# Two-layer decoder trunk: from a two-tile, two-layer order to a layer-by-layer order over nine tiles, with background weight conversion

## What is computed

```
for l in range(2):
    x = x + 0.5 * swiglu(rms_norm(x), ffn1)             # F1: 1024 -> 2816 -> 1024
    h = rms_norm(x); q, k, v, u = h @ w_in[l]           # M: 1280 columns
    x = x + cat(norm(window_attn(q, k, v)), norm(pool(u))) @ w_out[l]
    x = x + cross_attention(rms_norm(x), rms_norm(mem)) # 4 heads, 256 memory rows
    x = x + 0.5 * swiglu(rms_norm(x), ffn2)             # F2
return rms_norm(x)
```

## Time and profile before

| | |
|---|---|
| median of 6 runs | 6290.85 us |
| the profiled execution, its own time | 6285.33 us |
| span of its slowest core (core 5) | 6283.7 us (cores 6255.7 to 6283.7) |
| mean granted TensorE clock, all cores | 0.930 to 0.933 |
| TensorE busy | 5334.3 us, 85% of the span, 28528 matmuls |
| VectorE, ScalarE, GpSimd busy | 38%, 27%, 16% |
| DMA queue of SP, share of 16 engines | 40.9% |
| DMA queue of GpSimd, share of 16 engines | 11.5% |
| matmul waits for FFN slots that are cast at first use | 425.1 us |
| HBM read, written | 1005 MB, 104 MB |

### The profile page before, as it was taken

The page is one execution under the profiler, slowest core; times in us unless marked ns, Lnnn a source line. Parts: engine busy times, 40 slices in busy tenths (PEclk is TensorE's granted clock), DMA queues, the critical chain, the costliest instruction groups (busy, mean ns, idle before and its releaser), DMA issues.

```text
span 6283.7 us, 87478 instructions; the slowest of 8 cores (6255.7 to 6283.7 us)
## 1 busy us (share of the span) xinstructions
PE 5334.3 (85%) x28528; PEld 2782.1 (44%) x28528; DVE 2379.3 (38%) x4167; ACT 1690.3 (27%) x3070; POOL 978.5 (16%) x1154
## 2 busy tenths in 40 slices
PE   5555756696765999999999999999999999999988
PEld 2222322243322444445455555555555555555545
DVE  1231222141122354434445444344444354453452
ACT  1132111122212232223233233233332332332342
POOL 1111111111101112111122111111211111110111
PEclk9777878898877999999999999999999999999999
DMA  8534457545364445444455655555555555555554
GB/s 194 133 85 114 117 123 159 132 138 151 101 150 101 173 141 189 138 162 156 162 196 168 210 180 188 170 196 179 199 176 187 180 187 197 187 171 190 178 164 163
DMA packets 280504, 1019.35 MB, mean 162 GB/s; under 512 B 32336, under 2 KB 32704, under 8 KB 279808
## 3 DMA queue, kind: packets, MB, share of 16 engines
q1 hardware_dynamic: 239472, 870.52, 40.9%
q0 software_dynamic: 39440, 141.12, 11.5%
q10 hardware_dynamic: 1152, 2.10, 0.1%
HBM read 1005.22 MB, written 104.33 MB: 177 GB/s over the span
## 4 chain that ended last, share of the span: by engine, by line
PE 68%; DMA 12%; DVE 8%; issue 5%; ACT 5%; POOL 1%; DVEq 0%; ACTq 0%; POOLq 0%; SPq 0%
PE ps L328 68%; DMA sb_fr<-wf 7%; DVE sb_hM L421 2%; DVE sb_hF L421 2%; DMA sb_mr<-wx 2%; DMA sb_mr<-wm 1%; ACT sb_rst L148 1%; DMA wfb<-sb_fr 1%; ACT sb_sqf L148 1%; ACT sb_tmp L148 1%; DVE sb_x L501 1%; POOL sb_ach L393 1%; ACT sb_pT L148 1%; POOL sb_acc L393 0%; ACT L145 0%
## 5 line engine op out<-in xcount | busy, mean ns | idle before, releaser
L328 PE MATMUL ps<-sb_hF,sb_fr 128*128 128x384 bf16 (+1 forms) x14080 | 2718.0, 350 | 248.4 <-DMA sb_fr<-wf 197.5
L328 PEld LDWEIGHTS ps<-sb_hF,sb_fr 128*128 128x128 bf16 x14080 | 1394.9, 100 | 1476.3 <-issue 437.5
L328 PE MATMUL ps<-sb_act,sb_fr 128*128 128x384 bf16 (+1 forms) x7040 | 1421.9, 356 | 234.6 <-DMA sb_fr<-wf 227.6
L466 DVE TENSOR_TENSOR sb_act<-ps,sb_sg 128x384 bf16<-128x384 f32 (+1 forms) x880 | 524.0, 596 | 1917.0 <-PE ps L328 1425.9
L393 POOL TENSOR_TENSOR sb_acc<-sb_acc,sb_sqf 128x384 f32<-128x384 f32 (+2 forms) x592 | 644.3, 1091 | 3386.9 <-ACT sb_sqf L148 3378.7
L328 PEld LDWEIGHTS ps<-sb_act,sb_fr 128*128 128x128 bf16 x7040 | 700.8, 101 | 883.1 <-issue 368.7
L328 PE MATMUL ps<-sb_hM,sb_mr 128*128 128x384 bf16 (+1 forms) x4000 | 862.4, 355 | 165.2 <-DMA sb_mr<-wm 99.0
L148 ACT ACTIVATE sb_sg<-ps 128x384 f32<-128x384 f32 (+1 forms) x880 | 454.0, 519 | 1310.3 <-PE ps L328 1157.2
L328 PEld LDWEIGHTS ps<-sb_hM,sb_mr 128*128 128x128 bf16 x4000 | 398.0, 100 | 569.8 <-issue 295.5
L148 ACT ACTIVATE sb_sqf<-sb_x 128x384 f32<-128x384 f32 (+1 forms) x630 | 345.0, 553 | 1124.3 <-DVE sb_x L501 360.8
L148 ACT ACTIVATE sb_pT<-ps 128x512 bf16<-128x512 f32 (+2 forms) x452 | 234.1, 553 | 522.9 <-PE ps L328 520.8
(11 more groups left out here) (86 smaller groups left out, 2326.8 us busy)
## 6 DMA issues: line engine op xcount, KB each, us to landing
sb_fr<-wfb SPq DMA_DIRECT2D x1188, 512.0 KB, 4.1
sb_mr<-wmb SPq DMA_DIRECT2D x162, 512.0 KB, 5.2
sb_mr<-wab SPq DMA_DIRECT2D x160, 512.0 KB, 4.4
sb_fr<-wf POOLq DMA_DIRECT2D x132, 512.0 KB, 8.6
wfb<-sb_fr SPq DMA_DIRECT2D x132, 512.0 KB, 5.3
sb_mr<-wx POOLq DMA_DIRECT2D x32, 512.0 KB, 9.7
sb_x<-xT POOLq DMA_DIRECT2D x7, 1536.0 KB, 11.6
yT<-sb_x POOLq DMA_DIRECT2D x56, 192.0 KB, 6.5
```

What stands on the lines that cost most here:

```text
L328: P.op("pe", lambda h: h.matmul(out_ap, lt, rh, start=st, stop=sp_, skip_group_check=True), reads=list(rb), writes=(ob_,), signal=(i == n ...
L466: P.op("dve", lambda h: h.tensor_tensor(out=actF[:, hc, :T], in0=d[1][0][:, :T], in1=sg[si][:, :T], op=ALU.mult), (d[1][1], sgb[si]), (act ...
```

## The change

Tiles are now nine (six of 512 positions, three of 384), and the order is by layer: the 18 (layer, tile) units v = 0 to 17 run in one pipeline, whose stage v has F2 of unit v-1, M of unit v and F1 of unit v+1. Stage -1 is F1 of unit 0, stage 18 is F2 of unit 17. After layer 0 x goes to DRAM (`store_x`) and is loaded again for layer 1; the rope tables go the same way. F1 of every unit takes its norm statistics from x in `xs` (`prenorm_steps`), spread over the F2 down projection and the attention.

Only `wf[0]` (33 slots, F1 of layer 0) is still cast into the ring at first use. All other weights are cast DRAM to DRAM by `convert`, several slots per DMA on the POOL queue, and every load of them is a bf16 load on SP. `conv_first` (25 slots: wm 0 to 4, wx 0 to 15, wm 5 to 8 of layer 0) is issued at the end of stage -1, `conv_second` (33 slots, F2 of layer 0) spread over stage 0, and the 91 slots of layer 1 spread over stages 1 to 7. The DMAs that write `wab` get a semaphore for each ring slot.

```diff
-    n += n % 2
...
+    wxb_d = nc.dram_tensor("wxb", [L, 16, 128, SLOT], BF16, kind="Internal").ap()
+    x1_d = nc.dram_tensor("x1", [128, NCH, NT], F32, kind="Internal").ap()
+    tab_d = nc.dram_tensor("tab", [ntl, 2, 128, TT], F32, kind="Internal").ap()
...
-            if (a, s) not in fresh[kind]:
-                fresh[kind].add((a, s))
+            src, dst, buf = BANKS[kind]
+            if kind == "wf" and a == 0 and s not in fresh:
+                fresh.add(s)
                 P.dma("pool", slot[:, :], src[a, s], writes=(sb_,), box=swbox[rk][i])
...
+        def convert(kind, a, s0, s1):
+            src, dst, buf = BANKS[kind]
+            P.dma("pool", dst[a, s0:s1].rearrange("s p e -> (s p) e"), src[a, s0:s1].rearrange("s p e -> (s p) e"),
+                  writes=tuple(buf[a][s0:s1]), box=P.new_box(f"cv_{kind}{a}_{s0}"))
...
-            P.dma("pool", xs[s][:, :, :T], xT_d[:, :, c0:c0 + T], writes=tuple(xbs[s]), box=xbox[s])
+            s = v % NXS
+            src, rd = (xT_d, ()) if l == 0 else (x1_d, (x1buf[ti],))
+            P.dma("pool", xs[s][:, :, :T], src[:, :, c0:c0 + T], reads=rd, writes=tuple(xbs[s]), box=xbox[s])
+
+        def store_x(ti, l):
+            c0, T = tiles[ti]
+            s = (l * ntl + ti) % NXS
+            P.dma("pool", x1_d[:, :, c0:c0 + T], xs[s][:, :, :T], reads=tuple(xbs[s]), writes=(x1buf[ti],), box=xsbox[s])
...
+            if l < L - 1:
+                return [(lambda: store_x(ti, l), 0.1)]
...
+        conv_first = conv_list("wm", 0, 0, 5, 3) + conv_list("wx", 0, 0, 16, 4) + conv_list("wm", 0, 5, 9, 4)
+        conv_second = conv_list("wf", 1, 0, 33, 3)
+        conv_later = []
+        for l in range(1, L):
+            conv_later += conv_list("wf", 2 * l, 0, 33, 3) + conv_list("wm", l, 0, 9, 3) + conv_list("wx", l, 0, 16, 4) + conv_list("wf", 2 * l + 1, 0, 33, 3)
...
+        for v in range(-1, NV_T + 1):
+            M = tl(v) if 0 <= v < NV_T else None
+            F2 = tl(v - 1) if v - 1 >= 0 else None
+            F1 = tl(v + 1) if v + 1 < NV_T else None
...
+                fs += raw(gu2[:2]) + early
+                fs += merge(gu2[2:], seg1)
+                ps_, ph_ = prenorm_steps(*F1)
+                fs += sprinkle(merge(dn2, seg2), raw(ps_ + ph_))
+                fs += raw(gu1[:2])
...
+                fs += merge(gu1[2:], final_steps(*F2) + [(lambda v=v: load_x(v + 2), 0.1)] + segw + seg3)
+                d1, d2 = split_frac(dn1, 0.72)
+                fs += merge(d1, seg4)
+                fs += merge(d2, tail)
+                run(sprinkle(fs, bg))
```

More of the change, by code:

```diff
@@ L368, in load, with conv_list @@
                 flush_wb(rk, 0)
-                P.dma("sp", slot[:, :], dst[a, s], reads=(buf[a][s],), writes=(sb_,))
+                rd = tuple(buf[a][4:]) if kind == "wab" and s >= 4 else (buf[a][s],)
+                P.dma("sp", slot[:, :], dst[a, s], reads=rd, writes=(sb_,))
             return slot, sb_
+        def convert(kind, a, s0, s1):
+            src, dst, buf = BANKS[kind]
+            P.dma("pool", dst[a, s0:s1].rearrange("s p e -> (s p) e"), src[a, s0:s1].rearrange("s p e -> (s p) e"),
+                  writes=tuple(buf[a][s0:s1]), box=P.new_box(f"cv_{kind}{a}_{s0}"))
+        def conv_list(kind, a, s0, s1, step):
+            return [(lambda c=c: convert(kind, a, c, min(c + step, s1))) for c in range(s0, s1, step)]
+        conv_bg = []
         class Stat:
@@ L476, in f_dn @@
             T = tiles[ti][1]
-            stats[key] = Stat(NCH, D, T)
+            if key is not None:
+                stats[key] = Stat(NCH, D, T)
             st = {"cur": -1}
@@ L503, in res @@
                     ps_free(d["ps"])
-                    stats[key].add(x_, xb_)
+                    if key is not None:
+                        stats[key].add(x_, xb_)
                 steps.append((lambda g=mmd: g(0), mmw(11, T)))
@@ L548, in rope_table_steps @@
                     steps.append((lambda tbl=tbl, tb=tb: P.act(tbl[:, :T], a[:, :T], AF.Sin, (ab, constb), (tb,), bias=vcol(V_NPI)), 0.7))
+            for j, (tb, bb) in enumerate(((cos2[pr], cosb[pr]), (sinS[pr], sinb[pr]))):
+                steps.append((lambda tb=tb, bb=bb, j=j: P.dma("pool", tab_d[ti, j, :, :T], tb[:, :T], reads=(bb,), writes=(tabbuf[ti][j],), box=tabbox[pr * 2 + j]), 0.1))
             return steps
@@ new lines, in build_program @@
+                fs += merge(d1, seg4)
+                fs += merge(d2, tail)
+                run(sprinkle(fs, bg))
+            elif v == -1:
+                gu = f_gu(F1[0], F1[1], 1)
+                dn = f_dn(F1[0], F1[1], 1, ("mix", F1[0], F1[1]))
+                ps_, ph_ = prenorm_steps(*F1)
+                run(raw(ps_) + raw(ph_))
+                extra = [(late_consts, 0.1)] + ropes + [(lambda: load_x(1), 0.1), (lambda: load_x(2), 0.1)]
+                run(merge(gu, extra))
+                ps_, ph_ = prenorm_steps(*tl(1))
+                run(merge(dn, ps_ + ph_))
+                run(conv_first)
+            else:
@@ L1112, in build_program @@
+                fs = []
+                fs += raw(gu[:2]) + early
+                d1, d2 = split_frac(dn, 0.72)
+                fs += merge(gu[2:] + d1, seg1 + seg2 + segw + seg3 + seg4)
+                fs += merge(d2, tail)
+                if f == 2:
+                    if key is not None:
+                        fs.append(lambda key=key: stats[key].fin())
+                    fs += raw(final_steps(*Fx))
+                run(sprinkle(fs, bg))
         for bx in ybox:
```

199 lines of the change are left out of this document (70 added, 129 removed).

## The result

The changed kernel takes 5760.88 us (median of 10 runs, 5757.26 to 5770.35), the kernel before 6294.33 us in the 20 runs beside them. The ratio is 0.9153 [0.9146, 0.9161]: 8.5% faster, 534 us. The prediction was 5680 us with a range of 5590 to 5860, so the time lies in the range, 81 us above the forecast, and 21 us above the band of 5600 to 5740 that had most of the chance. The profiled execution took 5765.1 us by its own time, with a span of 5763.5 us on core 7 (the eight cores span 5724.0 to 5763.5).

What follows compares the result with a forecast made beforehand. TensorE was taken to bound stages without casts; stages 1 to 4 also paid cast waits and a lower clock. Terms 259 + 375 + 4726 + 43 + 270 = 5673 us, 611 under the span; off the median 5680, range 5590 to 5860.

Steps and rivals of the forecast that it cites:

- Stages 1 to 16: Full stages: 59 blocks of 128 positions at 80.1 us, the price of old stages without casts, 4726 us.
- Background conversion at nothing: Layer 1's 91 slots, 13 a stage and 46 us of 320, cost nothing beside weight loads, covered by the F ring.
- The slower rival: Stages 0 to 7: conversions stall TensorE as casts did, 149 slots at 4.9 us, 6350 us in all; chance 0.04.
- POOL as a gate: Nine stages storing x: the x load holds POOL until the store lands, TensorE loses 180 us, 5860 us; chance 0.07.
- The fourth rival: Full stages gain nothing from wider tiles: 59 blocks at 81.3 us, 71 us more, 5750 us; chance 0.10.
- Memory keys and values of layer 1: In stage 9: old stage 3 less 320 us less its 109 us of waits, 43 us.
- Stage -1: Start of the kernel: same tile, 33 casts and write-backs as the old stage 0, 259 us.
- Stage 0: Old stage 1's 432 us less 116 us of cast waits, 316, plus three additions: 347 to 395, taken as 375 us.
- second of the stage's three additions: Stage 0: wm 5 to 8, last of 25 slots, ready at 378 us, wanted at about 380: no wait; 35 us later at 4.9.
- The first addition: Start of stage 0: SP needs conv_first's first three slots, 11 to 15 us, and a load replaces the cast: +10 to +14.
- The third addition: Stage 0: two conv_second DMAs of three slots stand among the wab writes on POOL's queue, 21 to 29 us.
- The first rival: Starved start, stage 0: each load needs eight turns between conversion rows, 28 us; about 75 us later, 5755 us; chance 0.12.

Runs made afterwards that it cites:

- the run with two slots: Changed kernel with only slot 0 of wm and of wx of layer 0 converted in conv_first, all their loads reading it: ratio 0.8957 to before, 5665.36 and 5671.1 us.
- the first experiment: Changed kernel with conversion rows of 2048 elements (4 KB written) in place of 16384 (32 KB): 5760.53 us, ratio 0.9162 to before.

## Why the prediction was right, and where a step of it failed

- **Stages 1 to 16.** 59 blocks at 80.1 us and 43 for the memory: 4769 against 4771 measured. That the old stages without casts price the work itself held, and the granted clock is 0.98 over this whole window. That it held to 2 us is luck: without 20 us of waits for F loads (next item) and with the memory's 34 us for 43, the blocks cost about 4717, 9 less than forecast.
- **Background conversion at nothing.** Stages 1 to 3, which convert, took 315 to 318 us; stages 10 to 13, which don't, 317 to 318. In stage 4 TensorE waited 7.3 us for an F load, and in stages 5 to 7 3.3 to 4.7. That is some 20 us where the sum has nothing. The slower rival needed 4.5 us a slot over 149 slots; conv_first alone came near that, 4.3 us a slot over 23.
- **POOL as a gate.** Stages 1 to 3 store x and stages 10 to 13 don't, with no difference in time; in stage 1 ACT's Squares waited 2.4 us for POOL. The rival falls.
- **Wider tiles.** The fourth rival falls by the row of stage 10: 79.5 us a block.
- **Memory keys and values of layer 1.** Stage 9 is 34 us over stage 10, 43 forecast; 7 of the 34 were the `wab` writes.
- **Stage -1.** 4 us over, with 100.7 us of TensorE's waits for casts against 88.1.
- **Stage 0: the step that failed.** It is the price of the bf16 loads beside conv_first. The second of the stage's three additions lets 17 of them land among the conversions at some 1.4 us each, so that TensorE has its first half done by 380, wm 5 to 8 are there at 378, and there is "no wait". wm 5 to 8 were indeed not waited for. But the loads ahead of them landed 34 us apart, TensorE stood 108 us before three of them (51.6, 30.9 and 26.0) until 391, and the first output projection began at 467. The first addition, 10 to 14 us, has the same fault: the first three slots took 18.0 us, near its 11 to 15, but the load behind them some 40 where it has 4.1, and these make the wait of 51.6. Both together are what the run with two slots gave back, 98 us. The slot was mis-sized too: 5.0 us elapsed, and 4.6 of the engines' time (316 rows of 32 KB, 16 to a slot, in 94.7% of 95 us, as shown below), where the sum has 3.5. The third addition, 21 to 29 us for conversions among the `wab` writes, has the right size for another reason, and that is luck: the writes waited for one another, 24 us in stage 0 by the run that sets them apart. So 316 + 24 + 98 = 438; the 22 us left to 460 are also in the run with two slots (362 less 316 and 24), and were not taken apart.
- **The first rival is what stage 0 did.** It has eight turns of 3.5 us, 28 us a load, and 5755 us; measured were 34 us, eight turns of 4.2 us, and 5760.9. So the time is in the range because the range took in this rival. I gave it 0.12 because two queues shared the engines fairly in the earlier trace rows. But the casts there have rows of 4 KB, and so say nothing of rows of 32 KB. While the loads starved, from 292 to 387 us, the two queues show turns of one row each (packets, MB, share; the packets count some of 4 bytes):

```profile
q0 software_dynamic: 388, 10.35, 94.7%
q1 hardware_dynamic: 378, 1.42, 6.1%
```

10.35 MB are 316 rows of 32 KB and 1.42 MB are 346 rows of 4 KB, so about one row of a load for each row of a conversion. By the rule of the Trainium skill (DMA: Bandwidth & Descriptors, section SWDGE vs HWDGE vs iDMA), that an engine changes queue only at the end of a packet, the sum would have been that rival's; the trace agrees, with 34 us a load behind long rows and a load every 7 us or so behind short ones (310.63, 317.85 in the first experiment). In one thing the rival falls short, though: with short rows alone the time stayed, since of the 38 us that TensorE had won by the first output projection 24 went to the load of the memory, and the rest to smaller waits on both sides of it. What counts is how much conversion, and whatever else waits on its queue, stands ahead of what the stage needs next.

## What to carry to other kernels

Moving a cast into the background pays (570 us here) where whole stages lie between it and its use; the stages that hid it here had DMA shares of 0.57 to 0.77. At the start, where all is needed at once, it is on the path with nearly its full DMA time, 4.3 us a slot here; the corrections together got 81 us of stage 0 back, by converting first what is needed first, in short rows, with no small load behind it, and by moving some of it into the next stage, which paid 24. Before a queue's share is taken from a stretch of the trace, compare the length of the rows there with those of the new transfers. And when several writes come to name one buffer, ask whether the program now makes each wait for the one before: here twelve waits on one queue held a small load, that load held VectorE, and VectorE held TensorE; without them stages 0 and 9 are 31 us shorter.

## What the runs showed of the hardware that was not expected

- A weight load of 512 KB landed a median of 4.3 us after its issue over the span, and 34 us apart while conversions of 32 KB rows were queued on the other queue.
- A conversion from DRAM to DRAM of a slot (1 MB read, 0.5 MB written) took 5.0 us with the engines full and some loads in between, as much as a cast into SBUF and its write-back together (4.9 us).
- While conv_first ran, short rows brought a load every 7 us or so in the place of 34 and made the conversions slower, 145.7 us for 122.6, and the stage no shorter: of a lead of 38 us at the first output projection 24 went to the load of the memory, which took 38.8 us for 14.5 on the conversions' queue.
